# Banded attention by pairs of heads between quarter blocks of the value projection, late conditioning sums, gate rows through HBM

## What is computed

```python
kv = rmsnorm(h, kv_norm) @ w_kv                 # k and v, 1024 wide each
q = rmsnorm(h, b_norm) @ w_q
s = q_n @ k_band.T * scale + bias[rel]          # 256 tokens: the band is causal by chunks of 64
p = softmax(where(valid, s, NEG_INF))
h = h + (p @ v_band) @ w_out

mod = silu(c) @ w_mod + b_mod                   # 6 x 1024: sh1, sc1, g1, sh2, sc2, g2
x = x + g1 * (concat(ret, att) @ w_out)
x = x + g2 * (square(relu(h2 @ w_ff1)) @ w_ff2)
```

## Time and profile before

| | |
|---|---|
| median of 3 runs | 1186.64 us (1185.91 to 1189.78) |
| the profiled execution's own time | 1183.16 us |
| its span, first to last instruction | 1181.4 us |
| PE busy | 1094.8 us, 93% |
| DVE busy | 844.0 us, 71% |
| ACT busy | 596.3 us, 50% |
| POOL busy | 84.6 us, 7% |
| DMA | 192.46 MB, 163 GB/s on average |
| mean granted clock of PE | 0.963 |

### The profile page before, as it was taken

One profiled execution on the slowest core, in us unless ns is written; L12 is line 12 of the kernel. 1 busy time (PEld: TensorE's weight loads), 2 busy tenths in 40 slices (PEclk: granted clock), 3 DMA queues, 4 the chain that ended last, 5 costly groups with the idle time before them and its releaser, 6 DMA issues.

```text
span 1181.4 us, 20845 instructions
## 1 busy us (share of the span) xinstructions
PE 1094.8 (93%) x7586; PEld 1002.1 (85%) x7586; DVE 844.0 (71%) x1508; ACT 596.3 (50%) x1018; POOL 84.6 (7%) x99
## 2 busy tenths in 40 slices
PE   3999799899999999976899999999999897999996
PEld 3998799799999889975799999888867686999885
DVE  4895787677888877795489888566778645556554
ACT  4556232455656545436476666555444644445542
POOL 0103142110000000110000000001100100000000
PEclk9998898999999999986999999999999988999998
DMA  8474243168666785990456665644422124666551
GB/s 255 125 213 146 89 143 108 37 215 249 190 188 190 242 277 176 313 345 2 163 158 179 178 182 186 204 140 124 126 71 72 36 75 122 179 180 208 190 185 53
DMA packets 216592, 192.46 MB, mean 163 GB/s; under 512 B 6801, under 2 KB 194321, under 8 KB 216401
## 3 DMA queue, kind: packets, MB, share of 16 engines
q1 hardware_dynamic: 206832, 159.49, 44.9%
q0 software_dynamic: 8512, 31.99, 7.7%
q10 hardware_dynamic: 1184, 0.14, 0.1%
HBM read 190.55 MB, written 1.05 MB: 162 GB/s over the span
## 4 chain that ended last, share of the span: by engine, by line
PE 62%; issue 18%; DVE 10%; DMA 4%; ACT 4%; POOL 1%; DVEq 0%; SPq 0%; POOLq 0%; ACTq 0%
PE ps L539 17%; PE ps L541 17%; PE ps L540 17%; DVE wL L1785 2%; DMA modw<-in_w_mod_t 2%; PE ps L768 1%; DMA raw<-in_a_w_in 1%; PE ps L933 1%; PE ps L754 1%; DMA raw<-in_f_w_up 1%; PE ps L738 1%; DVE cv L1807 1%; ACT wH L1102 1%; PE ps L911 1%; PE ps L823 1%
## 5 line engine op out<-in xcount | busy, mean ns | idle before, releaser
L1785 DVE TENSOR_TENSOR wL<-raw,wH 128x1024 fp32r<-128x1024 f32 x298 | 355.4, 1221 | 117.1 <-ACT wH L1102 115.3
L1102 ACT ACTIVATE wH<-raw 128x1024 fp32r<-128x1024 f32 x298 | 309.4, 1058 | 230.8 <-PE ps L541 206.8
L539 PE MATMUL ps<-yH,wH 128*128 128x256 f32 x704 | 199.1, 283 | 0.3 <-DVE wL L1785 0.3
L540 PE MATMUL ps<-yL,wH 128*128 128x256 f32 x704 | 198.3, 282 | 0.0
L541 PE MATMUL ps<-yH,wL 128*128 128x256 f32 x704 | 198.3, 282 | 0.0
L539 PE MATMUL ps<-xH,wH 128*128 128x256 f32 x512 | 146.5, 286 | 2.4 <-DVE xL L1785 2.3
L540 PE MATMUL ps<-xL,wH 128*128 128x256 f32 x512 | 145.8, 285 | 0.0
L541 PE MATMUL ps<-xH,wL 128*128 128x256 f32 x512 | 145.7, 285 | 0.0
L539 PEld LDWEIGHTS ps<-yH,wH 128*128 128x128 f32 x704 | 132.7, 188 | 0.5 <-DVE wL L1785 0.5
L540 PEld LDWEIGHTS ps<-yL,wH 128*128 128x128 f32 x704 | 132.7, 188 | 0.1
L541 PEld LDWEIGHTS ps<-yH,wL 128*128 128x128 f32 x704 | 132.7, 188 | 0.0
(11 more groups left out here) (385 smaller groups left out, 1873.8 us busy)
## 6 DMA issues: line engine op xcount, KB each, us to landing
raw<-in_f_w_up SPq DMA_DIRECT2D x88, 512.0 KB, 4.7
raw<-in_w_ff SPq DMA_DIRECT2D x64, 512.0 KB, 4.1
modw<-in_w_mod_t POOLq DMA_DIRECT2D x48, 512.0 KB, 5.2
raw<-in_f_w_down SPq DMA_DIRECT2D x44, 512.0 KB, 4.3
raw<-in_a_w_in SPq DMA_DIRECT2D x32, 512.0 KB, 4.9
raw<-in_w_in SPq DMA_DIRECT2D x22, 512.0 KB, 3.8
raw<-in_w_kv SPq DMA_DIRECT2D x16, 512.0 KB, 4.8
raw<-in_a_w_out SPq DMA_DIRECT2D x8, 512.0 KB, 4.2
```

What stands on the lines that cost most here:

```text
L539: mm(o, l[0], r[0], start=first, stop=False, skip_group_check=check)
L540: mm(o, l[0], r[1], start=False, stop=False, skip_group_check=check)
L1102: fn(wH[:, c % SPLIT], raw[:, c % RAW], ACT.Copy).then_inc(hi_done, 1)
L1785: return tt(o, x, hi.bitcast(F32), ALU.subtract)
```

## The change

**Order.** The projections of step 2 run k, q, v; k and v now read their input from `x2H` and `x2L`, q from `xH` and `xL`.

**Attention.** It runs in eight pairs of heads, two in flight, each on two PSUM banks of its own. The value projection is cut into half units, and its units 2 to 7 lie between the steps of pairs 0 to 5; pairs 6 and 7 finish inside wo_b's first block. A pair's scores wait until DVE has split the result of the pair two before.

**Conditioning.** Eleven sums stand in `down0`, ten in `down1`, eight in `ff2`, none in the projections of step 2. The last 18 tiles have a ring of their own, `modw2`, in memory that is free by then.

**Gates.** Each gate is kept as columns. POOL stores it to HBM and loads it again onto all partitions; the row holds element (p, k) at 8 p + k, and the residuals read it at every eighth element.

The core of the diff, first the sums and PE's order:

```diff
+MOD_LATE = 30
+MODS_WITH = {"down0": (1, 3, 4, 5, 7, 9, 10, 11, 13, 15, 17), "down1": (0, 1, 3, 5, 7, 9, 11, 13, 15, 17), "ff2": range(2, 18, 2)}
...
+            def band_scores(i):
+                pe.wait_ge(bank_free, BANK["q"] + i // 2 + 1)
+                if i >= 2:
+                    pe.wait_ge(y_ready, BAND_Y + i - 1)
...
+            def values_and_band(x):
+                band_scores(0)
+                band_scores(1)
+                for u in range(2):
+                    for t in range(TT):
+                        v_half(u, t)
+                for i in range(BAND_PAIRS - 2):
+                    band_turn(i)
+                    v_half(i + 2, 0)
+                    band_y(i)
+                    v_half(i + 2, 1)
+                    band_scores(i + 2)
```

The same function on ACT:

```diff
+                band_exps(0)
+                band_exps(1)
+                hi(0, 8, U("v") + SPLIT)
+                hi(0, 8, U("v") + SPLIT + 1)
+                v_rows(0)
+                for i in range(BAND_PAIRS):
+                    band_turned(i)
+                    if 1 <= i < BAND_PAIRS - 1:
+                        band_exps(i + 1)
+                    band_hi(i)
+                    if i + 2 < BAND_PAIRS:
+                        hi(0, 8, U("v") + SPLIT + i + 2)
+                        if i % 2:
+                            v_rows((i + 2) // 2)
```

And on DVE:

```diff
+                maxima(0)
+                maxima(1)
+                probabilities(0)
+                lo(0, 8, U("v") + SPLIT)
+                lo(0, 8, U("v") + SPLIT + 1)
+                for i in range(BAND_PAIRS):
+                    if 1 <= i < BAND_PAIRS - 1:
+                        maxima(i + 1)
+                    turned_last(i)
+                    if i + 2 < BAND_PAIRS:
+                        lo(0, 8, U("v") + SPLIT + i + 2)
+                    if i + 2 == BAND_PAIRS:
+                        probabilities(i + 1)
+                    low(i)
+                    if i + 2 < BAND_PAIRS:
+                        probabilities(i + 1)
```

The gates, on POOL and then on DVE (`last_gate` stands behind the bodies of ff2):

```diff
+            def gate_store(g):
+                pool.wait_ge(gate_dve, g + 1)
+                pool.dma_start(gate_hbm[g].rearrange("(p k) -> p k", p=P), gate_cols[:, g]).then_inc(gate_out, 16)
+            def gate_load(g, o):
+                pool.wait_ge(gate_out, 16 * g + 16)
+                pool.dma_start(o[:], gate_hbm[g:g + 1].partition_broadcast(P).rearrange("p a n -> p (a n)")).then_inc(gate_in, 16)
...
+                    if name == "ff2":
+                        last_gate()
...
+                        if gate is not None:
+                            dve.wait_ge(gate_in, 32)
...
-                            st.do(tt(tmp, b, gate[:, c * 512:(c + 1) * 512], ALU.mult))
+                            st.do(tt(four(tmp), four(b), by_tiles(gate)[:, 4 * c:4 * c + 4], ALU.mult))
...
+            def by_tiles(gate):
+                return gate[:].rearrange("p (n k) -> p k n", k=KD)
```

More of the change, by code:

```diff
@@ new lines, in band_scores @@
+            def band_scores(i):
+                pe.wait_ge(bank_free, BANK["q"] + i // 2 + 1)
+                if i >= 2:
+                    pe.wait_ge(y_ready, BAND_Y + i - 1)
+                for x in range(2):
+                    q, k = qT[64 * x:64 * x + 64, i], kT[64 * x:64 * x + 64, i]
+                    b = ps[ATT_PAIR[i % 2][x]]
+                    mm(b[:, 0:256], q[:, P:], k, start=True, stop=True)
+                    last = mm(b[:, 256:384], q[:, 0:P], k[:, 0:P], start=True, stop=True)
+                last.then_inc(b_score, 1)
@@ new lines, in band_hi, with values_and_band, v_rows @@
+            def band_hi(i):
+                act.wait_ge(y_pe, BAND_Y + i + 1)
+                cp(xH[:, i], ps[ATT_PAIR[i % 2][1]][:, 256:512]).then_inc(y_hi, 1)
+            def values_and_band():
+                def v_rows(j):
+                    act.wait_ge(unit_done, U("v") + 2 * j + 2)
+                    b = ps[(BANK["v"] + j) % 4]
+                    for t in range(TT):
+                        last = fn(vt[:, t, j * 256:(j + 1) * 256], b[:, t * 256:(t + 1) * 256], ACT.Identity, scale=rstd[:, t:t + 1])
+                    last.then_inc(bank_free, 1)
+                act.wait_ge(rstd_done, STAT["kv"] + 1)
+                act.wait_ge(bank_free, BANK["v"])
+                st.wait(st.n)
+                band_exps(0)
[12 more added lines that the diff above has]
+                            v_rows((i + 2) // 2)
@@ L1909, in body @@
                     if gate is not None:
-                        st.do(tt(s, s, rep(gate[:, bass.ds((i * 4 + j) * 256, 256)], TT), ALU.mult))
+                        for t in range(TT):
+                            sk = s[:, t].rearrange("p (k n) -> p k n", k=2)
+                            st.put(tt(sk, sk, by_tiles(gate)[:, 2 * j:2 * j + 2], ALU.mult))
+                        st.wait(st.n)
                     tt(hc, hc, s, ALU.add).then_inc(unstaged, 1)
-                blocks(name, body, 1 if gate is not None else 0, after=after)
+                blocks(name, body, TT if gate is not None else 0, after=after)
             def added(name, n, gain, after=None):
@@ L2572, in _ @@
             dve.wait_ge(res_done, RES["x2"])
-            residual("wo_c", gate1)
+            dve.wait_ge(gate_in, 16)
+            residual("wo_c", gate2)
             dve.wait_ge(unstaged, STAGED["wo_c"] + 4)
```

306 lines of the change are left out of this document (140 added, 166 removed).

## The result

The changed kernel takes 1177.11 us (median of 10 runs, 1171.47 to 1182.08) against 1187.76 (10 runs, 1184.32 to 1189.78) for the kernel before: ratio 0.9912, 95% interval 0.9888 to 0.9935. It is faster by 0.9%, where I had forecast 1188.5. The profiled execution took 1177.84, its span is 1175.9.

A forecast was written before the change was run, and what follows sets the result against it. TensorE (PE) bounds the kernel; time is to be had only where it waits or runs slower. +2.3 - 3.0 + 1.8 + 0.8 = +1.9 on 1183.16 gives 1185.1; that execution lay 3.5 below the median, so 1188.5, range 1180.5 to 1193.

The forecast's parts named there:

- Interleaving +2.3: Value projection and banded attention: 72.6 us against 70.3 before, clock falls included, so 2.3 us slower.
- the ring: Interleaved attention: scores(i+2) wait for low(i), behind a split that waits for PE; PE idles 2.6 us in six turns.
- Gate-row matmuls -3.0: The eight gate-row records between 575.00 and 578.03 go, 3.0 us less.
- Sums moved, 0: Conditioning sums moved into both down projections and ff2 are covered by PE's work: cost 0.
- Late gate +1.8: Last residual: the second gate's store and load through HBM move the end by 1.2 to 3.2 us, taken as 1.8.
- Strided read +0.8: Last residual and wo_c: products reading the gate at every eighth element cost 0.8 us more, bounds 0 and 2.9.
- rival C: Slower: at the end, gates 3.2 us late and strided reads at double price, +5.4, 1192.0 us; chance 0.14.
- signs of being wrong: Wrong if attention gaps are below 1 us, gated products exceed 1 us, or PE waits for wL in a down projection.
- A: The forecast: PE stalls in the attention, clock falls in most turns, gate rows pay; 1184 to 1191 us; chance 0.53.
- B: Faster: attention stalls are there, but the clock holds through 2.6 us; -5.3, 1181.3 us; chance 0.22.
- D: Down projections: late sums hold up DVE or their fetches come late, 4.6 to 6.9 us more, 1193 to 1195; chance 0.05.
- E: Attention: the ring is looser, a turn nearer PE's own 5.4 us; 1165.7 us; chance 0.06.

The follow-up runs named there:

- before with the pad: The kernel before with 64 unused bytes per partition behind modc, no instruction changed: 1176.25 us, ratio 0.9909 to the kernel before.
- the changed kernel unshifted: The changed kernel with gate_cols laid over unused elements of rows_a, so every tile lies where it lay before: 1187.68 us, ratio 1.0018 to the kernel before.
- the run with the dense gate: Changed kernel with low(i) and probabilities ahead of the split, xH/xL moved, last gate's addition earlier, gate copied dense, pT_b copy ahead of maxima: 1148.95 us.
- the run with low first: The changed kernel with low(i) and probabilities(i+1) ahead of the split of unit i+6 in DVE's order: 1159.34 us, ratio 0.9762 to the changed kernel.
- the later one: The changed kernel run once more, nothing edited: 1185.48 us.
- the pair above: Changed kernel with low(i) first, xH/xL moved, last gate's addition earlier, profiled with and without the dense gate edits: executions 10.8 us apart, 1143.72 and 1154.53.

## Why the prediction was wrong

**The step that failed** is one that the sum never had. I priced a unit at 24 matmuls 0.12 apart and used the same price in both kernels, for every stage the diff leaves alone; I read `gate_cols` as an addition of DVE's and not as 64 bytes ahead of PE's operands. What the runs show in its place is a step of 113.3 or 117.8 ns for 118.7, and of 228.9 for 232.4, in stages that I had left out of the sum. No rival held it. That the step isn't one number stood in the earlier trace rows: 22.9 / 8 is 2.86 us a unit and not the 2.88 that I took, since q reads `x2H` at 118.7, not 120. By what path the distance acts no run shows. The Trainium skill ("TensorE: Matmul & The Clock Gate", Step-by-step: what each phase is for) says that loading the next weights takes no read bandwidth from the running matmul, by which the distance of the two operands should make no difference. Here it made one, 120.0 against 113.3 ns at one clock; the measurement decides. The shift was worth 10.4 us by the medians (before with the pad), more than any term of the sum. By the first profiles: `up0` and `down0` 4.7, `up1` and `down1` 2.0, `ff2` 1.3, k 1.0 (it now reads `x2H`, and would have kept 120.0 on `xH`).

**The rest of the sum** is tested by the changed kernel unshifted: +1.0 us by the medians, where it said +1.9. That this is so near is in part luck. The profiled executions, 1188.31 and 1183.16, differ by 5.2, which the measured terms below make up (5.9 - 3.0 + 2.5 = 5.4): the interleaving's term was too small, the two at the end were off by 0.8 and 0.7 against each other, and the attention of the first profile was a quick one:

- Interleaving +2.3. The order of the ring, its releaser and the six waits were right; in the changed kernel a turn takes 10.0 to 10.2 instead of 9.6, the wait 2.89 instead of 2.6. From `down0` to `up1` the unshifted kernel needs 151.64 us, as the window below shows, against 148.71, so +2.9 with the gate rows' -3.0 in it: the term is +5.9. But these 148.71 hold the attention at 47.3; in four other profiles of the same attention code it took 49.1 to 50.6. Against those the term is +2.6 to +4.1.
- Gate-row matmuls -3.0: these matmuls are gone and nothing takes their place in `wo_b`.
- Sums moved, 0: right. PE is at 100% in both down projections, as the two windows of the changed kernel show. Its one wait for `wL`, 1.76 us at 280.97, is in `up0`, where there are no sums; why it arises there isn't shown.
- Late gate +1.8: the first gated product came about 1.0 us behind the end of its half. The two DMAs of the last fence below, issued at 1154.77 and 1156.72, took 1.7 and 4.2 us. By the Trainium skill ("DMA: Bandwidth & Descriptors", Anatomy of one DMA) I had estimated 2.0 and 3.2, in time: near for the store, too short for the load.
- Strided read +0.8: the product took 1.17 and 1.06 instead of 0.69, four times, so about 1.5. Together 2.5 for 2.6; rival C's double price didn't come. But a product over 1 us was one of my own signs of being wrong, and it came: 0.8 spread over four products would have made them 0.9. In the run with the dense gate the products were back at 0.69, so the extra was the way the gate is read. That run took away the stride and the split into four pieces at once; the piecewise operation of the earlier trace rows, no dearer than a dense one, speaks for the stride. By the Trainium skill ("SBUF — State Buffer", Door 1: The DMA port swizzle) each access that crosses to a new line pays; these products agree.

```profile
449.84:601.48 151.64, 129.22 (x978) 121.89 (x976) 81.64 (x186) 72.80 (x166) 3.11 (x5) 0.92 0.43 133
```

```profile
409.00:425.00 16.00, 16.00 (x72) 13.13 (x71) 13.46 (x21) 8.19 (x12) 2.12 (x4) 1.00 0.94 332
748.00:764.00 16.00, 16.00 (x71) 13.15 (x70) 12.32 (x19) 7.72 (x13) 1.58 (x3) 1.00 0.88 325
```

```profile
gate<-gate_rows POOLq DMA_DIRECT2D x1, 512.0 KB, 4.2
gate_rows<-gate_cols POOLq DMA_DIRECT2D x1, 4.0 KB, 1.7
```

**The rivals.** A's mechanism happened and its number, 1188.5, is met by the unshifted kernel at 1187.68, in part by the luck just named. B fell: the clock fell behind each of the six waits of 2.89 us. C: the end cost 2.5, not 6.1. D: no. E: not as written, but one reordering, the run with low first, brings its short turn (6.7 us, for E's 5.4) and 17.8 us.

**What stays open.** What decides between 113.3 and 117.8 at the same distance. The step holds for dozens of units. In the first profile of the changed kernel it went from 113.3 to 117.8 in `up1` where PE leaves the units to turn the context's rows, with a wait of 1.27 us; in the run with the dense gate it didn't, at the same place. With the tiles as in the changed kernel `down0` ran at 228.9 wherever `up0` had ended at 113.3, and at 233.3 where it had ended at 117.8, but `down1` behind an `up1` at 117.8 ran at either. That the spread of the changed kernel, 10.6 us in ten runs and 14.0 with the later one, comes from this is argued from its two profiles and the pair above, not shown; 17 later runs of the kernel before spread over 8.3. Why the attention of before takes 47.3 in some executions and 50 in others is open too, but for the clock that goes with it, and so is why the clock falls behind a wait of 1.97 us in one execution and holds in another.

## What to carry to other kernels

Before crediting a gain to an edit, count matmuls in windows of untouched stages: if a fully busy window at the same clock holds more of them, the operands have moved relative to each other, and a kernel with only the new allocation settles it in one run. Pad tiles so that moving and stationary operands don't lie at the same place modulo 256 bytes; here 64 bytes apart was best, for 512 columns only with the moving operand past the other, and unused memory alone gave 1.4%. Read the addresses of the built kernel: a pad may be rounded up. Where an in-order engine holds both a ring's next split and a small result that PE waits for, put the small result first.

## What the runs showed of the hardware

- Float32r matmuls of 128 x 128 by 256 columns, each with its own weight load, started every 113.3 to 120.0 ns at a granted clock of 1.00, by the distance of their operands in memory modulo 256 bytes; of 512 columns every 228.9 to 233.3. The distance counts with its sign (32: 116.7 or 117.8, -32: 118.3), an address by itself doesn't.
- At one distance there can be two steps, each held for dozens of units: 113.3 and 117.8 at 64 and at -64, 116.7 and 117.8 at 32, 117.3 and 118.7 at -96.
- An elementwise product whose second operand is read at every eighth element took 1.05 to 1.17 us for 512 elements instead of 0.69.
- In the changed kernel a wait of PE of 2.89 us was followed by a fall of the clock each time, six times of six; with low first, waits of 0.99 to 1.12 us, five in a row, by none. Behind a wait of 1.97 us the clock held in one execution of the changed kernel and fell in the other.
